# A hybrid decoder layer on one core: its triangular inverses built from 32x32 diagonal blocks instead of 64x64 ones

## The reference, cut to what matters

```
a_mat = jnp.where(strict, kk * dec * bc[..., :, None], 0.0)
sol = lax.linalg.triangular_solve(eye + a_mat, rhs, left_side=True, lower=True, unit_diagonal=True)
u_mat, w_mat = sol[..., :dv], sol[..., dv:]
delta = u_mat - jnp.einsum('bhid,bhdv->bhiv', w_mat, s)
```

## Time and profile before

| | |
|---|---|
| median of 3 runs | 826.42 us (826.28 to 826.58) |
| span of the profiled execution, first to last instruction | 824.0 us |
| PE matmul busy | 805.6 us, 98% of the span |
| DVE, ACT, POOL busy | 403.4, 214.9, 152.6 us |
| stage from the first lY to the first gV on PE | 241.98 to 270.56 us |

### The profile page before, as it was taken

The page is one execution under the profiler, slowest core; times in us unless marked ns, Lnnn a source line. Parts: engine busy times, 40 slices in busy tenths (PEclk is TensorE's granted clock), DMA queues, the critical chain, the costliest instruction groups (busy, mean ns, idle before and its releaser), DMA issues. The chain is left out here.

```text
span 824.0 us, 12898 instructions
## 1 busy us (share of the span) xinstructions
PE 805.6 (98%) x5184; PEld 506.9 (62%) x5184; DVE 403.4 (49%) x883; ACT 214.9 (26%) x469; POOL 152.6 (19%) x182
## 2 busy tenths in 40 slices
PE   9999999999999999999999999999999999999995
PEld 4545777887889987777777776455433333334443
DVE  3223457584667522664854458836352101104976
ACT  3211152329224311131101110122121111125275
POOL 0234321004046133300220034000100001004100
PEclk9999999999999999999999999999999999999999
DMA  9520364312020110504232122234899999995211
GB/s 361 209 102 1 111 205 154 107 67 86 26 72 35 41 65 14 204 19 156 103 153 69 85 103 103 80 121 178 303 407 354 422 430 419 402 401 206 77 52 64
DMA packets 20976, 135.23 MB, mean 164 GB/s; under 512 B 2436, under 2 KB 3076, under 8 KB 13748
## 3 DMA queue, kind: packets, MB, share of 16 engines
q1 hardware_dynamic: 13328, 103.08, 32.2%
q0 software_dynamic: 4720, 23.83, 7.9%
q10 hardware_dynamic: 2868, 7.47, 2.8%
HBM read 118.94 MB, written 19.63 MB: 168 GB/s over the span
## 5 line engine op out<-in xcount | busy, mean ns | idle before, releaser
L818 PE MATMUL pair<-mem 128*128 128x288 f32 x640 | 158.9, 408 | 0.0
L818 PEld LDWEIGHTS pair<-mem 128*128 128x128 f32 x640 | 120.3, 190 | 35.6 <-ACT mem L1508 2.1
L988 PE MATMUL single<-mem 128*128 128x288 f32 x448 | 110.0, 407 | 0.3
L988 PEld LDWEIGHTS single<-mem 128*128 128x128 f32 x448 | 84.7, 190 | 25.7 <-issue 1.6
L1375 PE MATMUL single<-mem 128*32 128x512 f32 x768 | 85.1, 594 | 0.9 <-DVE mem L2534 0.9
L1508 ACT ACTIVATE mem<-pair 128x512 f32<-128x512 f32 (+5 forms) x83 | 36.5, 487 | 162.6 <-PE pair L818 63.1
L1508 ACT ACTIVATE mem<-single 128x256 f32<-128x256 f32 (+5 forms) x109 | 44.6, 419 | 126.8 <-PE single L1236 48.5
L1375 PEld LDWEIGHTS single<-mem 128*32 128x32 f32 x768 | 23.6, 110 | 52.8 <-issue 51.7
L2527 DVE SCALAR_TENSOR_TENSOR mem<-single,mem 128x256 f32<-128x256 f32 x12 | 5.8, 485 | 102.3 <-PE single L1375 91.1
L1227 PE MATMUL pair<-mem 128*128 128x512 f32 x112 | 51.0, 601 | 0.0
L1444 PE MATMUL pair<-mem 128*128 128x512 f32 x112 | 49.4, 595 | 0.3 <-issue 0.3
(11 more groups left out here) (431 smaller groups left out, 1120.9 us busy)
## 6 DMA issues: line engine op xcount, KB each, us to landing
mem<-in_w_gu SPq DMA_DIRECT2D x17, 2048.0 KB, 14.1
mem<-in_w_down SPq DMA_DIRECT2D x17, 1024.0 KB, 13.5
y_slots<-mem SPq DMA_DIRECT2D x9, 512.0 KB, 9.7
y_slots<-in_zeros POOLq DMA_DIRECT2D x8, 512.0 KB, 8.4
mem<-in_w_ga SPq DMA_DIRECT2D x2, 2048.0 KB, 8.3
mem<-in_w_gb SPq DMA_DIRECT2D x2, 2048.0 KB, 7.7
mem<-in_w_wo SPq DMA_DIRECT2D x2, 2048.0 KB, 7.8
mem<-in_w_pg SPq DMA_DIRECT2D x2, 2048.0 KB, 17.9
```

What stands on the lines that cost most here:

```text
L818: last = nc.tensor.matmul(pb[:, hf, 0:HALF], w(k), rhs[:, k, hf * HALF:(hf + 1) * HALF], start=(k == 0), stop=(k == kk - 1))
L988: last = nc.tensor.matmul(single[plan.buf[s]][:, 0:HALF], lhs[:, k, :], rhs[:, k, :], start=(k == 0 and j in (0, 1, 3, 4)), stop=(k == 3), ...
```

## The change

Levels 2 to 16 now work on diagonal blocks of 32: 128 partitions hold four of them ("strips"), and each head has 32 columns. For a head and prompt tile there are four matmuls, each with a 32x32 weight and 32 columns, in the four diagonal positions of the array. Masks, X, Y and XD have half as many columns. The masked buffers become 8. Level 32 has no mask and no packed X: products of blocks, from one strip to its neighbour, with `A32` kept apart, write straight into `X64` (the 64-blocks) and `XT`. Level 64 keeps its 64x64 products. `XT` and `X64` are zeroed whole on POOL. `gA` has 7 ACT copies for a prompt tile (4 strips, 2 of A32, 1 of A21). The diagonal of `XT` is filled by ACT in a new step `lD`: 4 copies for each prompt tile after the four lY of level 32, 2 copies for the sample tile after the lY of level 8. POOL copies two strips per prompt tile from X to X64 after lX of level 16. Level 1 moves from POOL to DVE for its last part: DVE now masks, subtracts and transposes. The core of the diff:

```diff
-    for s in [1] + LEVELS[:-1]:
-        r, l = p[:, None] % 64, p[None, :64]
+    for s in [1] + LEVELS[:-2]:
+        r, l = p[:, None] % 32, p[None, :32]
...
-        s += [("lA", v, t) for t in on if v < 64] + [("lY", v, t) for t in on]
+        s += [("lA", v, t) for t in on if v < 32] + [("lY", v, t) for t in on]
+        s += [("lD", 4)] if v == 8 else [("lD", t) for t in on] if v == 32 else []
         for t in on:
-            if v != levels(t)[-1]: s += [("lX", v, t)]
-            if not by_blocks(v, t): s += [("lT", v, t)]
+            if v < 64: s += [("lX", v, t)]
+            if v >= 32: s += [("lT", v, t)]
...
-        blocks = lambda t: [slice(64 * b, 64 * b + 64) for b in range(2 if t < 4 else 1)]
+        strips = lambda t: [slice(32 * b, 32 * b + 32) for b in range(ntok(t) // 32)]
-            return view(base, H, 64, n=ntok(t))
+            return view(base, H, 32, n=ntok(t))
...
                         for h in range(H):
-                            for r in blocks(t):
+                            for r in strips(t):
                                 last = nc.tensor.matmul(out[r, h, :], am[r, h, :], X[t][r, h, :], start=True, stop=True)
+                    elif v == 32:
+                        for h in range(H):
+                            for r, to in zip(strips(t)[0::2], strips(t)[1::2]):
+                                last = nc.tensor.matmul(out[to, h, :], A32[t][r, h, :], X[t][r, h, :], start=True, stop=True)
                     else:
+                        pe.wait_ge(sem("x64"), 2 * t + 2)
                         for h in range(H):
-                            last = nc.tensor.matmul(out[64:P, h, :], A21[t][:, h, :], X[t][0:64, h, :], start=True, stop=True)
+                            last = nc.tensor.matmul(out[64:P, h, :], A21[t][:, h, :], X64[t][:, h, :], start=True, stop=True)
...
-                            for r in blocks(t) if v < 32 else blocks(t)[0:1]:
+                            for r in strips(t) if v < 32 else strips(t)[1:2]:
                                 last = nc.tensor.matmul(out[r, h, :], XD[t][r, h, :], Y[t][r, h, :], start=True, stop=True)
...
-                            for r in blocks(t):
-                                last = nc.tensor.matmul(out[r, h, :], Y[t][r, h, :], XD[t][r, h, :], start=True, stop=True)
+                            for to, r in zip(strips(t)[0::2], strips(t)[1::2]):
+                                last = nc.tensor.matmul(out[to, h, :], Y[t][r, h, :], XD[t][r, h, :], start=True, stop=True)
...
                     src = heads(s, n, n)
-                    for r in blocks(t):
+                    for r in strips(t):
                         last = copy(AD[t][r], src[r, :, r])
                     if t < 4:
+                        for r, to in zip(strips(t)[0::2], strips(t)[1::2]):
+                            copy(A32[t][r], src[r, :, to])
                         last = copy(A21[t], src[0:64, :, 64:P])
...
-                elif k0 == "lT" and s[1] == 32:
-                    t = s[2]
-                    ev_wait(act, s)
-                    for r in blocks(t):
+                elif k0 == "lD":
+
+                    t = s[1]
+                    act.wait_ge(sem("l1T"), blocks_done(16 if t < 4 else 4, t))
+                    act.wait_ge(sem("xt_zero"), t + 1)
+                    for r in strips(t):
                         last = copy(XT[t][r, :, r], XD[t][r])
                     last.then_inc(sem("diag"), 1)
...
+                elif k0 == "lX" and s[1] == 16:
+
+                    t = s[2]
+                    ev_wait(pool, s)
+                    pool.wait_ge(sem("xt_zero"), t + 1)
+                    for r in strips(t)[0:2]:
+                        G.tensor_copy(X64[t][r, :, r], X[t][r]).then_inc(sem("x64"), 1)
```

More of the change, by code:

```diff
@@ L92, in second_half @@
     return ("x2c" if POS[t] == 3 else "x2b", t)
-def by_blocks(v, t):
-    return v < 32 and v != levels(t)[-1]
 def blocks_done(v, t):
-    order = [(w, u) for w in LEVELS for u in range(NT) if w in levels(u) and by_blocks(w, u)]
+    order = [(w, u) for w in LEVELS if w < 32 for u in range(NT) if w in levels(u)]
     return NT + 1 + order.index((v, t))
@@ L122, in constant_tables @@
     c["before"] = (p[:, None] < p[None, :]).astype(f)
[L123 to L124 removed]
+    for s in [1] + LEVELS[:-2]:
+        r, l = p[:, None] % 32, p[None, :32]
         c[f"lev{s}"] = ((r // (2 * s) == l // (2 * s)) & ((r // s) % 2 == 0) & ((l // s) % 2 == 1)).astype(f)
[L126 to L127 removed]
+    c["ident4"] = np.tile(np.eye(32, dtype=f), (4, 1))
     g = np.array(GAMMA, np.float64)
@@ L471, in build @@
         E = [hb(E_[t], t, P) for t in range(NT)]
-        blocks = lambda t: [slice(64 * b, 64 * b + 64) for b in range(2 if t < 4 else 1)]
+        strips = lambda t: [slice(32 * b, 32 * b + 32) for b in range(ntok(t) // 32)]
         def packed(base, t):
-            return view(base, H, 64, n=ntok(t))
+            return view(base, H, 32, n=ntok(t))
         AD = [packed(AT_[t], t) for t in range(NT)]
+        A32 = [view(AT_[t] + 128, H, 32) for t in range(4)]
         A21 = [view(AT_[t] + 256, H, 64, n=64) for t in range(4)]
         X = [packed(X_[t], t) for t in range(NT)]
+        X64 = [view(X_[t] + 256, H, 64, n=64) for t in range(4)]
         Gr = [hb(X_[t], t, P) for t in range(NT)]
@@ L482, in build @@
         Y = [packed(Y_[t], t) for t in range(NT)]
-        XD = [packed(Y_[t] + 256, t) if t < 4 else XT[t] for t in range(NT)]
-        masked = [slot(32) + 256 * i for i in range(4)]
+        XD = [packed(Y_[t] + 128, t) for t in range(NT)]
+        Y64 = [view(Y_[t] + 256, H, 64) for t in range(4)]
+        masked = [slot(32) + 128 * i for i in range(8)]
         U_ = [(slot(0 + t) if t < 4 else slot(34)) for t in range(NT)]
@@ L1100, in _ @@
                     t, n = s[1], ntok(s[1])
-                    ev_wait(pe, ("lT", levels(t)[-1], t))
                     if t < 4:
-                        pe.wait_ge(sem("diag"), t + 1)
+                        ev_wait(pe, ("lT", 64, t))
+                    pe.wait_ge(sem("diag"), t + 2 if t < 4 else 1)
                     pe.wait_ge(sem("bek"), t + 1)
@@ L1683, in _ @@
                     mm_wait(act, s)
-                    r = slice(0, n) if v < 64 else slice(64, P)
-                    copy(Y[t][r], heads(s, n, 64)[r]).then_inc(ev(k0), 1)
-                elif k0 == "lT" and s[1] == 32:
-                    t = s[2]
-                    ev_wait(act, s)
-                    for r in blocks(t):
+                    if v < 32:
+                        last = copy(Y[t], heads(s, n, 32))
+                    elif v == 32:
+                        for r in strips(t)[1::2]:
+                            last = copy(Y[t][r], heads(s, n, 32)[r])
+                    else:
+                        last = copy(Y64[t][64:P], heads(s, n, 64)[64:P])
+                    last.then_inc(ev(k0), 1)
+                elif k0 == "lD":
[3 more added lines that the diff above has]
+                    for r in strips(t):
                         last = copy(XT[t][r, :, r], XD[t][r])
@@ L2131, in _ @@
                     ev_wait(dve, ("gA", t))
[L2132 to L2138, removed]
+                    link(V.tensor_tensor(XD[t], AD[t], bh(C("lev1", n), n, 32), ALU.mult))
+                    V.tensor_tensor(XD[t], bh(C("ident4", n), n, 32), XD[t], ALU.subtract).then_inc(sem("l1T"), 1)
+                    dve.wait_ge(sem("l1T"), t + 1)
+                    V.transpose(X[t].rearrange("p h w -> p (h w)"), XD[t].rearrange("p h w -> p (h w)")).then_inc(sem("l1X"), 1)
                 elif k0 in ("lX", "lT"):
@@ L2142, in _ @@
                     mm_wait(dve, s)
-                    src = heads(s, n, 64)
+                    src = heads(s, n, 32 if v < 64 else 64)
                     if v == 64:
                         last = V.tensor_scalar(XT[t][0:64, :, 64:P], src[0:64], -1.0, None, ALU.mult)
-                    elif k0 == "lX":
+                    elif k0 == "lT":
+                        dve.wait_ge(sem("xt_zero"), t + 1)
+                        for r, c in zip(strips(t)[0::2], strips(t)[1::2]):
+                            last = V.tensor_scalar(XT[t][r, :, c], src[r], -1.0, None, ALU.mult)
+                    elif v == 32:
+                        dve.wait_ge(sem("xt_zero"), t + 1)
+                        last = V.tensor_scalar(X64[t][32:64, :, 0:32], src[32:64], -1.0, None, ALU.mult)
+                    else:
                         if v == 2:
                             dve.wait_ge(sem("l1X"), t + 1)
[L2149 to L2152, removed]
+                        last = V.tensor_tensor(X[t], X[t], src, ALU.subtract)
                     last.then_inc(ev(k0), 1)
-                    if by_blocks(v, t):
+                    if v < 32:
                         ev_wait(dve, s)
@@ L2837, in _ @@
                     t, n = s[1], ntok(s[1])
-                    pool.wait_ge(sem("l1m"), t + 1)
```

(7 more changed lines are left out.)

21 lines of the change are left out of this document (11 added, 10 removed).

## The result

The change made the kernel slower: 845.96 us (median of 4 runs, 845.5 to 846.54) against 826.35 us (826.23 to 826.58), a ratio of 1.0233 with a 95% interval of 1.0221 to 1.0246. The forecast was 820.3 us. The profiled execution took 846.54 us and has a span of 844.7 us, 20.7 more than the earlier trace rows; the medians of the runs differ by 19.6. The 1.1 us between the two is scatter of the two profiled executions: wherever the record has both numbers of an execution, its time lies 1.8 to 2.0 us over its span, not the 2.4 us that I had taken from a median and a span of different executions.

A forecast was written before the change was run, and what follows sets the result against it. PE bounds the kernel, nearly equal with DVE in the stage. 4.8 us gained up to level 16 (gA's loss included) and 1.3 behind: 6.1 off 824.0, span 817.9, plus 2.4 gives 820.3 us; range 817.0 to 827.0.

The forecast's parts named there:

- the part on records: PE in the inverse stage: 1,248 small records plus the old 64 of level 64, each small one taken at 10 ns.
- first rival: Instruction issue bounds PE: small records still cost 29 ns over a long run, time 840.1 us; issue as bound, slower: 0.15.
- The 60 cycles: Skill's overhead per matmul, estimated as 25 ns a record: small records would cost 31.2 us, time about 835 us.
- gA: Ahead of level 2: the fifth gA waits for the first one's ACT copies; PE loses 0.8 us, level 2 starts at 242.8.
- DVE's turn: Levels 4 to 16: DVE's pair of operations, subtract and transpose, falls from 0.785 to 0.53 us a tile.
- ACT's lD: Levels 32 and 64: 16 copies at 0.33 us, 5.3 us in all, ahead of the copy that level 64's lT needs.
- the new bound: ACT bounds levels 32 and 64: PE stands some 2 us; the stretch takes 9.8 us against 11.1 before.
- POOL's masks: Levels 4 to 16: smaller masks run ahead and hide behind DVE's 0.53 us a tile; otherwise at most 0.15 us a tile.
- The second rival: ACT's mostly fixed-cost copies eat the gain: 2.7 us gained, 823.7 us; copies or clock, alone or together, leaving 0-3 us: 0.23.
- The third, the clock: Grant falls to 1.2 GHz around level 64: at most 3 us lost, 823.3 us; shares the 0.23 with ACT's copies.

The follow-up runs named there:

- the split kernel: The kernel before, each 64-column product of levels 2 to 32 issued as two matmuls of 32 columns with the same weights: 880.67 us, ratio 1.0654.
- the blocks that wait for nothing: The kernel before plus 256 independent 32x32-weight matmuls ahead of projection rg 2, with 32, 64 or 128 columns: 840.84, 839.04 and 841.62 us.
- the kernel before with the spread projections: The kernel before, projections rg 2 and 3 cut into 16 parts, one behind every second product of a tile: 846.01 us, ratio 1.0251.
- the block with 64 columns: The kernel before plus 256 independent matmuls of 32x32 weights and 64 columns ahead of projection rg 2: 839.04 us.
- the block with 32 columns: The kernel before plus 256 independent matmuls of 32x32 weights and 32 columns ahead of projection rg 2: 840.84 us.

## Why the prediction was wrong

**The step that failed** is in the part on records: "I take 10 ns, since a record now streams half the columns of those that took 14." The 10 ns are right for a burst: 10.0 measured in level 2. I multiplied them by 1,248. Over the whole of levels 2 to 32 a record costs 37.65 us / 1,248 = 30 ns. All I had were bursts of 16, which are filled from what PE has at hand. The prediction named this as its first rival and gave it 0.15; its mechanism was the right one, its price (29 ns) was the old matmuls' own and agrees with the feed's by coincidence. That it was their own shows in the first loads of level 2 before the change, which had been fetched under the projections: (1.94 - 0.134) / 63 = 29 ns.

```profile
241.98 1.94 PEld L1064 LDWEIGHTS single<-mem 64*64 64x64 f32 x64 [0.39 <-issue]
```

That rival forecast 840.1 us. From there to 846.0 are mainly the 4.3 us that level 64 and gV lose at half clock, which stood in another rival, as if the two excluded each other. They don't: the clock fell at the end of the first long stop. The old stage, whose longest gap on PE is 0.28 us, kept it full.

**What the trace of before could have said.** With 704 records in 24.4 us, 35 ns each with all waits, the old stage was already close to the feed's 30, so the 29 ns that I put down to the array needed a second look: the first loads above, and not the average, tell that it is the products' own. The old stage also has a stop for "issue" of 0.3 us. The instruction queue's rows (six packets from 240 to 272 us in the kernel before) were there to be asked. The Trainium skill, Runtime: NRT & Kernel Launch, section "Instruction fetch mechanics", says that instructions come in 16 KiB blocks of 256 and that this is mostly hidden, since dispatch is slower than the fill. The block size agrees with the 16 KB packets and the 128 records between stops; that it is hidden doesn't hold here, where PE took 128 records in 1.3 us and a block came every 3.5 to 4.0.

**The 60 cycles.** The Trainium skill, TensorEngine Tiling, section "Instruction Overhead", gives about 60 cycles of overhead for each matmul, which I had turned into an estimate of 25 ns. This is not what limits here: 8.5 to 10 ns a record were measured in the bursts. Its advice against taking a factor from a small dimension was right all the same, for another reason.

**gA** was forecast to cost 0.8 us, and PE's load waits 1.17 us there instead of 0.28, 0.9 longer. **DVE's turn** was forecast at 0.53 us a tile; subtractions of level 2 start 0.52 to 0.56 us apart in the first burst. It is right, and hidden. **ACT's lD**, 16 copies at 0.33 us: they take 5.12 us, 0.32 each, and they end at 285.84. PE comes to level 64's lT at 286.34, only just after the first copy behind them, so the new bound that I saw there did not come to bear; it would have at full clock (see above). The row, then the four copies of level 64 behind it, from ACT's timeline:

```profile
280.72 5.12 ACT L1512 ACTIVATE mem<-mem 32x128 f32<-32x128 f32 x16
285.86 1.20 ACT L1512 ACTIVATE mem<-single 64x256 f32<-64x256 f32 x4
```

**POOL's masks** (0.438 us each) stayed hidden as said. **The second rival**, ACT's copies, did not occur. **The third, the clock**, did: 3 us were forecast for it and 4.3 lost at half clock in level 64 and gV (of which the clock alone would give back some 2.9, by the estimate above), without what it did inside the stops, where it costs little since the feed is slower (at half clock 75 small records take 1.23 us, 13 ns each).

What stays open: how much the clock costs in all. No kernel kept the small records and full clock, so its price is read from stretches at both levels and not from a run that differs in the clock alone. Why the clock stays low through the 73 gapless microseconds of the split kernel, and comes back during gV, isn't shown either. Nor is what a block's 3.5 to 4.0 us are made of.

## What to carry to other kernels

A PE stage has a price in instructions beside its price in columns. Count loads and matmuls, and compare the stage with what the instruction queue brings: here 256 per 3.5 to 4.0 us, so that a float32 matmul of the program (four instructions) should occupy PE for 60 ns or more on average once one to two blocks are used up. Cutting a matmul into smaller ones that run side by side pays only above that. A price taken from a short burst must not be multiplied by the length of a long run.

## What the runs showed of the hardware that I had not expected

- Instructions for PE arrive in 16 KB packets, 256 loads and matmuls each, with restarts 3.85 us apart in the changed kernel and 3.5 to 4.0 in the blocks that wait for nothing. In such a block 195 records went before the first stop; in the changed kernel 253.
- A 2 MB weight load at the same time made a stop 4.6 us long instead of 2.1.
- Behind a stop the granted clock was at 0.5 for 41 us in the changed kernel, with further stops in between, and for 78 us in the split kernel, after one stop of 1.1 us and although PE was shown as busy without a gap for 73 of them, with small matmuls. In both it was back at full 3 to 5 us after the work changed to 128x128 weights. In the kernel before with the spread projections it fell at a stop of 1.5 us too, but came back after 6.8 us, while 64x64 products still ran.
- Not every stop does it: in the block with 64 columns the clock stayed at full through three stops of 0.9, 1.5 and 2.0 us. In the block with 32 columns it fell during the second of its stops, of 2.2, 2.5 and 1.5 us. What decides this isn't shown.
- A group of 4 wide records between small ones at full clock takes 1.17 us from start to start, against 0.98 in a row of them (4 x 0.245).
